# Low-rank decay columns joined to the output gate's, GLA values joined to MoBA values, and a new order of the projection's units

## The reference, cut to what matters

```
IN_LAYOUT = (('gla_q', 128), ('gla_k', 128), ('gla_v', 256), ('gla_r', 256), ('gla_a', 16),
    ('swa_q', 256), ('swa_k', 128), ('swa_v', 128), ('moba_q', 256), ('moba_k', 256), ('moba_v', 256),
    ('ret_q', 128), ('ret_k', 128), ('ret_v', 256), ('ret_g', 256), ('gates', 4096))

p = split_columns(rms_norm(h, ln1_g) @ w_in)                 # (512, 1024) @ (1024, 6928)
log_a = log_sigmoid(p['gla_a'] @ w_a2 + b_a) / 16            # (512, 16) @ (16, 128)
b = cumsum(log_a) in chunks of 64;  q_dec = q exp(b);  k_dec = k exp(-b)
o_gla = norm(masked(q_dec k_dec^T) v + q_dec state) * silu(p['gla_r'])
q, k of retention: rotate(q), rotate(k) with cos and sin tables
o_ret = norm(decayed(q k^T) v + ...) * silu(p['ret_g'])
h = h + (sum_i sigmoid(gate_i) * (o_i @ w_branch[i])) @ w_out
h = h + HierMoE(rms_norm(h))
```

## Time and profile before

| | |
|---|---|
| times of three executions | 1409.37, 1409.44, 1412.75 us, median 1409.44 |
| profiled execution | span 1408.3 us from first to last instruction; the median execution lies 1.1 us above this span |
| PE busy | 1351.1 us, 96% of the span |
| DVE, ACT, POOL busy | 445.5, 443.3 and 486.8 us, 32%, 31% and 35% |
| mean granted TensorE clock | 0.989 |
| transfers | 330.60 MB, 235 GB/s in the mean |

### The profile page before, as it was taken

How to read it: one execution, slowest core, us unless ns; L and a number is a source line. 1 busy time by engine, 2 the same in 40 slices (tenths; PEclk the granted TensorE clock), 3 DMA queues, 4 the chain that set the end, 5 groups by cost and what they waited for, 6 DMA issues and landing times.

```text
span 1408.3 us, 18760 instructions
## 1 busy us (share of the span) xinstructions
PE 1351.1 (96%) x7496; PEld 934.2 (66%) x7496; DVE 445.5 (32%) x989; ACT 443.3 (31%) x810; POOL 486.8 (35%) x241
## 2 busy tenths in 40 slices
PE   8999999999999999988999999999999999998986
PEld 7888877888887533333488888778888874333333
DVE  3352754111323421111333637430003243121114
ACT  5522576222232211111253326752223321111112
POOL 3634323565750111111154443337566401111101
PEclk9999999999999999999999999999999999999999
DMA  8422222234288999999972132123344889999997
GB/s 279 165 91 90 76 76 75 75 112 148 99 261 321 383 419 420 419 420 416 402 264 92 60 123 76 55 71 104 107 140 138 277 328 413 419 420 420 419 414 303
DMA packets 136338, 330.60 MB, mean 235 GB/s; under 512 B 16630, under 2 KB 98630, under 8 KB 113722
## 3 DMA queue, kind: packets, MB, share of 16 engines
q1 hardware_dynamic: 127610, 313.68, 59.3%
q0 software_dynamic: 8640, 15.69, 2.9%
HBM read 311.56 MB, written 33.55 MB: 245 GB/s over the span
## 4 chain that ended last, share of the span: by engine, by line
PE 78%; DMA 13%; DVE 3%; SPq 2%; ACT 2%; issue 1%; POOL 0%; DVEq 0%; POOLq 0%; ACTq 0%
PE ps L595 18%; PE ps L597 18%; PE ps L596 18%; PE ps L1017 13%; DMA w<-in_w 12%; SPq L488 2%; PE ps L813 1%; PE ps L820 1%; PE ps L799 1%; DMA yb<-y_dram 1%; PE ps L1009 1%; PE ps L910 1%; PE ps L632 1%; PE ps L1029 1%; PE ps L762 1%
## 5 line engine op out<-in xcount | busy, mean ns | idle before, releaser
L595 PE MATMUL ps<-uH,ringH 128*128 128x512 f32 x704 | 275.4, 391 | 0.0
L597 PE MATMUL ps<-uH,ringL 128*128 128x512 f32 x704 | 274.1, 389 | 0.0
L596 PE MATMUL ps<-uL,ringH 128*128 128x512 f32 x704 | 274.0, 389 | 0.0
L1017 PE MATMUL ps<-w,xT 128*64 128x512 f32 x1024 | 230.8, 603 | 11.3 <-DMA w<-in_w 10.6
L1017 PEld LDWEIGHTS ps<-w,xT 128*64 128x64 f32 x1024 | 78.7, 139 | 157.7 <-issue 152.3
L1464 POOL TENSOR_TENSOR ringL<-raw,ringH 128x2048 fp32r<-128x2048 f32 x28 | 128.7, 4606 | 82.2 <-ACT ringH L1168 82.2
L1017 PE MATMUL ps<-w,hT 128*64 128x512 f32 x512 | 123.1, 624 | 28.9 <-DMA w<-in_w 17.1
L597 PEld LDWEIGHTS ps<-uH,ringL 128*128 128x128 f32 x704 | 132.2, 188 | 27.6
L595 PEld LDWEIGHTS ps<-uH,ringH 128*128 128x128 f32 x704 | 132.2, 188 | 27.5
L596 PEld LDWEIGHTS ps<-uL,ringH 128*128 128x128 f32 x704 | 132.2, 188 | 27.2
L1512 POOL TENSOR_TENSOR ringL<-raw,ringH 128x2048 fp32r<-128x2048 f32 x32 | 147.4, 4605 | 4.8 <-ACT ringH L1316 4.8
(11 more groups left out here) (293 smaller groups left out, 1936.6 us busy)
## 6 DMA issues: line engine op xcount, KB each, us to landing
w<-in_w SPq DMA_DIRECT2D x176, 1024.0 KB, 18.4
raw<-in_w_in SPq DMA_DIRECT2D x53, 1024.0 KB, 5.4
w<-in_w SPq DMA_DIRECT2D x32, 512.0 KB, 18.8
raw<-in_w_out SPq DMA_DIRECT2D x8, 1024.0 KB, 5.4
yb<-y_dram SPq DMA_DIRECT2D x8, 1024.0 KB, 15.2
braw<-in_w_branch SPq DMA_DIRECT2D x24, 256.0 KB, 4.7
h_dram<-hs SPq DMA_DIRECT2D x2, 2048.0 KB, 11.2
y_dram<-attT SPq DMA_DIRECT2D x8, 512.0 KB, 9.1
```

Of the source, the lines that this page charges most:

```text
L595: mm(o, h, rh, start=first, stop=False)
L596: mm(o, h, rl_, start=False, stop=False)
L597: return mm(o, l, rh, start=False, stop=last)
L1017: ins = mm(o[r], lhs[:, r], rhs[x], start=first, stop=last, skip_group_check=True)
```

## The change

1. The first unit is now the 272 columns of the output gate and the low-rank columns together (`gr` 512 to 767, `ga` 768 to 783), which lie side by side in `w_in`. It fills slot 0 and the first 128 columns of slot 1 (`front`). Its four halves are of a new kind G: one token tile stationary, 272 columns moving, 24 matmuls. The unit and the half of `ga` are gone (`UNITS` has no unit 1), 24 halves instead of 23.
2. As the low-rank values now come out with tokens on the partitions, they are kept in `lgT` (`front_out` on ACT), transposed on PE (`rank_turn`), copied to `zaT`, and multiplied by `wa2`, of which four copies are loaded, in four matmuls of 16 x 128 x 128 instead of one of 16 (32 with the low part) x 128 x 512.
3. The GLA values and MoBA values are multiplied together as a D pair (units 5 and 6, 4 halves of 24 matmuls of 512) instead of four R halves in two places.
4. The order: gate and low rank, `sk`/`sv`, `rq`/`rk`, `gq`/`gk`, values, `rv`/`rg`, `sq`, `mq`, `mk`. Retention's values, gates and unrotated q and k have their own tiles (`rvv`, `rsr`, `rT`). GLA's pieces stand later: scores 7 to 10, chunk_kv 8 to 14, mix_out 10 to 16, out_transposes 12 to 18; retention's: scores 15 to 19, chunk_kv 17 to 20, mix_out 18 to 21, out_transposes 20 to 23. `rotate` moves from 13 to 16, directly behind `head_norm(0)`. `step(0)` moves from 20 of 23 to 23 of 24, so that all later steps fall into the branches.
5. The splits stand at the halves named in `SPLIT_AT`. The constants are loaded behind units 2 and 3 instead of behind unit 1, 12 transfers for 10. Two `bfill` transfers of branch 0 wait for later halves.

```diff
-UNITS = [("gv", 256), ("ga", 128), ("gr", 256), ("gq", 256), ("sq", 256), ("sk", 256), ("rq", 256),
-         ("rv", 256), ("rg", 256), ("mq", 256), ("mk", 256), ("mv", 256)]
-U_GATE, U_OUT, U_ALL = 12, 28, 32
+UNITS = {0: ("gr", 272), 2: ("sk", 256), 3: ("rq", 256), 4: ("gq", 256), 5: ("gv", 256), 6: ("mv", 256), 7: ("rv", 256),
+         8: ("rg", 256), 9: ("sq", 256), 10: ("mq", 256), 11: ("mk", 256)}
+U_GATE, U_OUT, U_ALL = 12, 28, 31
-HALVES = [("R", 0, 0, "gv"), ("R", 0, 1, "gv"), ("T", 1, 0, "ga"), ("R", 2, 0, "gr"), ("R", 2, 1, "gr"),
-          ("T", 3, 0, "gq"), ("T", 3, 128, "gk"), ("T", 4, 0, "sq"), ("T", 4, 128, "sq"), ("T", 5, 0, "sk"),
-          ("T", 5, 128, "sv"), ("T", 6, 0, "rq"), ("T", 6, 128, "rk"), ("D", 7, 0, "rvg"), ("D", 7, 1, "rvg"),
-          ("D", 8, 2, "rvg"), ("D", 8, 3, "rvg"), ("T", 9, 0, "mq"), ("T", 9, 128, "mq"), ("T", 10, 0, "mk"),
-          ("T", 10, 128, "mk"), ("R", 11, 0, "mv"), ("R", 11, 1, "mv")]
+HALVES = [("G", 0, 0, "gra"), ("G", 0, 1, "gra"), ("G", 0, 2, "gra"), ("G", 0, 3, "gra"), ("T", 2, 0, "sk"), ("T", 2, 128, "sv"),
+          ("T", 3, 0, "rq"), ("T", 3, 128, "rk"), ("T", 4, 0, "gq"), ("T", 4, 128, "gk"), ("D", 6, 0, "gvm"), ("D", 6, 1, "gvm"),
+          ("D", 6, 2, "gvm"), ("D", 6, 3, "gvm"), ("D", 8, 0, "rvg"), ("D", 8, 1, "rvg"), ("D", 8, 2, "rvg"), ("D", 8, 3, "rvg"),
+          ("T", 9, 0, "sq"), ("T", 9, 128, "sq"), ("T", 10, 0, "mq"), ("T", 10, 128, "mq"), ("T", 11, 0, "mk"), ("T", 11, 128, "mk")]
-N_CST = 10
-STEP0 = 20
+SPLIT_AT = {3: 3, 5: 4, 6: 5, 8: 6, 10: 7, 12: 8, 15: 9, 17: 10, 19: 11, 21: 12, 22: 13}
+SLOTS_OF = {6: slice(1, 3), 8: slice(0, RING, RING - 1)}
+N_CST = 12
+STEP0 = 23
@@ PE: the halves and pieces
-                if name == "ga":
+                if q == 4:
                     for k in range(KD):
-                        for y in (uH, uL):
-                            last = mm(ps[0:32, b * 512:(b + 1) * 512], ringH[:, s, 32 * k:32 * (k + 1)], y[:, k, :],
-                                      start=k == 0 and y is uH, stop=k == KD - 1 and y is uL)
+                        mm(bank(b), wH[:, k, off:off + P], uH[:, k, :], start=k == 0, stop=False)
+                        mm(bank(b), wH[:, k, off:off + P], uL[:, k, :], start=False, stop=False)
+                    pe.wait_ge(unit_low.h, unit_low.at(lay, nth(u)))
+                    for k in range(KD):
+                        last = mm(bank(b), wL[:, k, off:off + P], uH[:, k, :], start=False, stop=k == KD - 1)
...
+                    if q == 1 and lay:
+                        second_tile()
+                    hold(pe, rows_low.h, rows_low.at(lay, 2 * q + 1))
+                    for k in range(KD):
+                        if q == 2 and k == 4 and lay:
+                            norm_transposes(3, rows_low)
...
+                        last = mm3(bank(b, n), uH[:, k, tmc(off)], uL[:, k, tmc(off)], wH[:, k, :], wL[:, k, :], k == 0, k == KD - 1)
+            def rank_turn():
+                pe.wait_ge(bank_freed[0].h, bank_freed[0].at(lay, 2))
+                pe.wait_ge(bank_freed[1].h, bank_freed[1].at(lay, 2))
+                nc.tensor.transpose(bank(A[1], P), lgT[:], ident).then_inc(decay_arg.h, 1)
+
             def log_decay():
-                pe.wait_ge(bank_freed[0].h, bank_freed[0].at(lay, 2))
+                pe.wait_ge(decay_log.h, decay_log.at(lay, 1))
                 pe.wait_ge(s_cst.h, 16 * N_CST)
-                mm(bank(A[0]), wa2[:, lay, :], zaT[:], start=True, stop=True).then_inc(decay_arg.h, 1)
+                for t in range(NT):
+                    r = slice(32 * t, 32 * t + 16)
+                    last = mm(bank(A[t], P), wa2[r, lay, :], zaT[r, :], start=True, stop=True)
+                last.then_inc(decay_arg.h, 1)
-            PIECES = {3: log_decay, 7: lambda: scores(0), 8: lambda: chunk_kv(0), 10: lambda: mix_out(0),
-                      11: window_values, 12: lambda: out_transposes(0), 15: lambda: scores(1), 17: lambda: chunk_kv(1),
-                      18: lambda: mix_out(1), 20: lambda: out_transposes(1)}
+            PIECES = {4: rank_turn, 5: log_decay, 6: window_values, 10: lambda: scores(0), 14: lambda: chunk_kv(0), 16: lambda: mix_out(0),
+                      18: lambda: out_transposes(0), 19: lambda: scores(1), 20: lambda: chunk_kv(1),
+                      21: lambda: mix_out(1), 23: lambda: out_transposes(1)}
@@ ACT
+            def front_out(q):
+                bank_full(q)
+                fn(sr[:, q, :], bank(q % 2, 256), ACT.Silu)
+                fn(rank_in[:, q, 0:16], bank(q % 2)[:, 256:272], ACT.Copy).then_inc(bank_freed[q % 2].h, 1)
@@ ACT, start of layer 1 (layer 0: front_out(0), norm_h(2), norm_h(3), front_out(1), split_h(2))
                 row_squares(3)
+                split_h(2)
+                front_out(0)
                 norm_h(3)
+                front_out(1)
             act.wait_ge(squares_summed.h, squares_summed.at(lay, NT))
-            split_h(1)
...
-            for q in range(NH):
+            for q in range(2, NH):
                 kind, u, off, name = HALVES[q]
-                if (q == 0 and lay) or (q and HALVES[q - 1][1] != u):
-                    split_h(u + 2)
+                if q in SPLIT_AT:
+                    split_h(SPLIT_AT[q])
@@ POOL
-                q = (4, 16)[br]
-                hold(pool, bank_freed[0].h, bank_freed[0].at(lay, q // 2 + 1))
-                hold(pool, bank_freed[1].h, bank_freed[1].at(lay, q // 2))
+                q = (3, 17)[br]
+                for b in range(2):
+                    hold(pool, bank_freed[b].h, bank_freed[b].at(lay, q // 2 + 1))
...
-                if q == 0 or HALVES[q - 1][1] != u:
-                    split_l(u + 2)
+                if q == 0:
+                    split_l(2)
+                if q in SPLIT_AT:
+                    split_l(SPLIT_AT[q])
                 if q == 0:
                     gp_.memset(attT[:].rearrange("p h t i -> p (h t i)"), 0.0).then_inc(att_cleared.h, 1)
-                if q in (4, 16):
-                    gain(q // 16)
-                if q in (10, 18):
-                    head_scale(q // 18)
+                if q in (7, 18):
+                    gain(q // 18)
+                if q in (16, 21):
+                    head_scale(q // 21)
@@ DVE, inside the loop over q
-                if q in (10, 18):
-                    head_norm(q // 18)
-                if q in (12, 20):
-                    out_low(q // 20)
+                if q in (16, 21):
+                    head_norm(q // 21)
+                if q in (18, 23):
+                    out_low(q // 23)
-                if q == 13:
+                if q == 16:
                     rotate()
@@ SP, branch 0
                 gate_fill(c + 2, U_GATE + c + 2)
+                if c == 0:
+                    hold(sp, bank_filled.h, bank_filled.at(lay, NH - 1))
+                elif c == 1:
+                    hold(sp, mix_turned.h, mix_turned.at(lay, 4))
                 bfill(0, c)
```

More of the change, by code:

```diff
@@ L257, in trunk @@
     s_init = signal("s_init", 0)
-    w_in_slot = [signal(f"w_in_slot{s}", 16 * 8) for s in range(RING)]
+    w_in_slot = [signal(f"w_in_slot{s}", 16 * (8 - (s == 1))) for s in range(RING)]
     unit_high = signal("unit_high", U_ALL)
@@ L415, in _ @@
                     fill(u, w_in_cols(lay, COL[name], n), slot)
-                if lay == 0 and u == 1:
+                if lay == 0 and u == 3:
                     constants()
@@ L680, in half @@
                 else:
[L681 to L696, removed]
-                            last = mm3(ps[:, b * 512 + i * n:b * 512 + (i + 1) * n], uH[:, k, tmc(2 * off + i)],
-                                       uL[:, k, tmc(2 * off + i)], wH[:, k, :], wL[:, k, :], k == 0, k == KD - 1)
@@ L737, in chunk_kv @@
                         last = mm(ps[DK * h:DK * (h + 1), b * 512 + n * DV:b * 512 + (n + 1) * DV],
-                                  k2[r, t, DK * h:DK * (h + 1)], vv[r, t, DV * h:DV * (h + 1)], start=True, stop=True)
+                                  k2[r, t, DK * h:DK * (h + 1)], values[br][r, t, DV * h:DV * (h + 1)], start=True, stop=True)
                 last.then_inc(kv_filled.h, 1)
@@ L1195, in _ @@
                 act.wait_ge(cst_in.h, 32)
[L1196 removed]
+                fn(front(ringH, 0, 1), front(raw, 0, 1), ACT.Copy).then_inc(front_high.h, 1)
                 row_squares(1)
@@ L1210, in _ @@
                 row_squares(3)
+                split_h(2)
+                front_out(0)
                 norm_h(3)
+                front_out(1)
             act.wait_ge(squares_summed.h, squares_summed.at(lay, NT))
-            split_h(1)
-            if lay == 0:
-                norm_h(2)
-                norm_h(3)
-                split_h(2)
             def k2_rows(br):
@@ new lines, in _ @@
+                    fn(rvv[:, off, :], bank(q % 2)[:, 256:512], ACT.Copy).then_inc(bank_freed[q % 2].h, 1)
+                elif name == "gvm":
+                    bank_full(q)
```

(24 more changed lines are left out.)

194 lines of the change are left out of this document (95 added, 99 removed).

## The result

| | before | changed |
|---|---|---|
| median of the runs side by side | 1411.07 us | 1425.22 us (1421.80 to 1426.04) |
| ratio, 95% interval | | 1.0096 [1.0084, 1.0109] |
| span of the profiled execution | 1408.3 us | 1423.5 us |
| mean granted TensorE clock | 0.989 | 0.985 |

Slower by about 14 us, beyond the upper end of the range, 1422.

What follows compares the result with a forecast made beforehand. PE was taken as the bound, 78% of the chain that ended last. Terms -10.1, +1.2, +2.0, +10.2, +3.0 and 0 sum to +6.3: span 1414.6, median 1415.7 us; range 1411 to 1421, or 1406 to 1422 with B and half of C.

Steps and rivals of the forecast that it cites:

- PE's work: PE's products in the projection, both layers: 5.1 us less a layer, -10.1 in all (bounds -10.9 and -8.5).
- D: Rival on the values' matmuls: the wide form does not pay, 2.8 us more, 1418.5; chance 0.03.
- Start of layer 1: G half 2 needs bank 0, freed late by front_out(0) on ACT: PE waits 1.2 us, once.
- GLA's decay chain: Scans, gain(0) and split_l(6) run late, so PE waits 1.0 us a layer before half 10: 2.0 in all.
- Rotate: From M, mix_out(0)'s end: POOL's split_l(11) delays DVE's rotate; PE waits 5.1 us a layer at second scores, 10.2 in all.
- A: Faster rival at rotate: it does not meet the split, wait 0.4 us, no clock loss, 1403.3; chance 0.14.
- B: Rival of about the same time: the wait at rotate is 3 to 4 us or the clock holds, 1408 to 1412; chance 0.16.
- C: Slower rival at rotate: POOL's gain(1) takes the turn before head_norm's product, about 3.6 us a layer, 1423; chance 0.07.
- The clock behind the wait: After the wait for rotate PE runs at a granted clock of 0.50, costing 1.5 us a layer, 3.0 in all.
- Steps: Attention steps: one 0.8 us wait goes, another of about the same size comes; zero, between -0.8 and +1.5.
- The chance of 0.60: Chance given to the forecast itself, the 5.1 us rotate wait with clock loss, own range 1411 to 1421.

Runs made afterwards that it cites:

- run 4: Changed kernel with gain(0) behind the split of unit 6 and, in layer 1, front_out(0) earlier on ACT: 1420.01 us, ratio 1.0069.
- Run 1: Changed kernel with the split of unit 11 one half later, at half 20 instead of 19: 1412.37 us, ratio 1.0013.
- run 2: Changed kernel with 20 keep-warm products of 128 columns on PE before it waits for rotate: 1415.05 us, ratio 1.0034.
- run 5: Idle PE instructions ahead of expert pairs: 80 a layer in the changed kernel, 1419.40 us, ratio 1.0062; 49 in the kernel before, 1416.62 us, ratio 1.0049.
- run 3: Changed kernel with 64 more wait instructions at the start of PE's program: 1428.81 us, ratio 1.0135.

## Why the prediction was right in direction and too low

- **PE's work**: -5.1 a layer forecast, -4.9 read. The four decay products took 0.44 us and the transpose 0.03 (35.04 to 35.07), for 0.45 forecast; that was a choice between 0.2 and 1.3 without a row, and it hit by luck. The 96 products of the values took 22.0 us (71.70 to 93.67), as forecast, 1.4 a layer less than the narrow form; D falls.
- **Start of layer 1**: forecast 1.2, measured 1.3, and gone with `front_out(0)` early (run 4). **GLA's decay chain**: the eight scans ended 8.1 us after their start, under `split_l(5)` and `gain(0)`; half 10 waited 1.0 us. Moving `gain(0)` removed it in run 4, in layer 0 as the only edit.
- **Rotate**: last product forecast at M+22.5, wait 5.1; measured M+22.4 and 5.0. Run 1 shows the cause, the split on POOL. Two small errors cancelled: the split began at M+15.55 instead of M+15.3 and took 4.95 instead of 4.6, and five of DVE's eight products were through before it instead of four. A, B and C fall: the collision came in both layers, and `head_norm`'s product kept its turn (115.06, `out_transposes(0)` at M+11.06).
- **The clock behind the wait**: mechanism right (run 2), size wrong. The term was 1.5 us a layer, from the one wait of the earlier trace rows; it measured 2.9 and 2.7, together 2.6 us more. In the earlier trace rows the clock was back some 3.5 us after PE went on; behind `rotate` it stayed low for 6.2 in layer 0 and 5.5 in layer 1. The window that follows that of the earlier trace rows, kernel before:

```profile
606.00:608.00 2.00, 2.00 (x10) 0.68 (x8) 0.00 (x0) 0.00 (x0) 0.00 (x0) 0.80 1.04 422
```

  0.80 of two microseconds leaves 0.8 us at half clock, to 606.8. The gap at the hand-over of the changed kernel had the same short form, 700.9 to about 703.8:

```profile
703.00:705.00 2.00, 2.00 (x6) 1.09 (x5) 0.49 (x1) 0.00 (x0) 0.00 (x0) 0.81 1.07 432
```

  I took one row as the price where it was only one of two sizes. What decides between the two is open; all runs with the wait untouched had score products of 1.9 to 2.1 us.
- **Steps**: forecast 0 within -0.8 and +1.5, read +0.5 a layer. Two waits of 0.26 and 0.34 us stand where one of 0.42 stood; the other 0.3 was not located.
- **The step that failed** is the sum, as a list of what the change touches. It counted PE's instructions only as time, and in "Start of layer 1" only ACT's order. It had no term for where the change moves PE's code: 209 and 194 instead of 160 and 96, with 5.3 us, the largest part of the error (run 5 gives 4.8 of them back, and puts such gaps into the kernel before). With that, the 2.6 of the clock and the 1.0 of the steps, 1415.7 becomes 1424.6; measured 1425.2, as the median lies 1.7 above the profiled span instead of 1.1. The page of before had the queue of the instructions and no gap, and a count of the added and removed instructions would have shown that the place moves. The chance of 0.60 was given to a mechanism that came true, in a range that had no room for what it left out.

## What to carry to other kernels

A long operation on POOL in the middle of a chain of DVE's products costs its whole length if PE waits for the chain: move the split, not the chain. Here it was one number in a list and worth 12 us. Price a wait of PE with the clock behind it, from more than one row.

A change that adds or removes PE instructions moves every later piece of program. Where PE jumps while the transfers run at full rate, look for "issue" in PE's waits, and shift the landing place with a few idle instructions before judging the change: here 5 us of the 14 came from where the code lay and not from the work that was edited. A comparison of two kernels can carry such a difference either way.

## What the runs showed of the hardware that was not expected

- The gap behind the jump was 0.9 to 4.3 us by landing place, in both kernels and both layers; at the hand-over of the changed kernel the clock behind it cost 1.3 us more.
- The clock stayed at 1.2 GHz for 2.9 and 3.5 us after PE went on from waits of 2.6 and 3.8 us, and for 6.2 and 5.5 us after the two waits of 4.9.
- A stream shuffle on DVE took its usual 0.77 us under a POOL product, while the product of two SBUF tiles behind it took 1.44 instead of 0.68.
- An idle wait instruction on PE cost about 0.15 us, an estimate from the 64 of run 3.
